# Cached MLA latents: read from a second, host-turned copy page by page, in place of turning them on TensorE

## The reference, cut to what matters

```python
past_c = cache_kv_latent[l][page_table].reshape(Bd, past_len, KV_LORA)   # 8 x 2048 x 128
past_r = cache_k_rope[l][page_table].reshape(Bd, past_len, A_ROPE)       # 8 x 2048 x 32
q_lat = einsum('bqhd,chd->bqhc', q_nope, w_uk)
s_past = (einsum('bqhc,bkc->bhqk', q_lat, past_c)
          + einsum('bqhr,bkr->bhqk', q_rope, past_r)) * scale
p = softmax(concat([s_past, s_new]))
o_lat = einsum('bhqk,bkc->bqhc', p[..., :P], past_c) + einsum('bhqk,bkc->bqhc', p[..., P:], c_new)
```

## Time and profile before

| | |
|---|---|
| median of 3 runs | 2114.58 us (2110.43 to 2116.58) |
| the profiled execution's own time | 2110.66 us |
| its span, first to last instruction | 2108.9 us |
| mean granted clock of PE | 0.995 |
| PE busy, of the span | 2081.8 us (99%) |
| DVE busy | 1573.1 us (75%) |
| ACT busy | 1285.1 us (61%) |
| DMA engines' mean rate | 228 GB/s |

### The profile page before, as it was taken

The page is one execution under the profiler, slowest core; times in us unless marked ns, Lnnn a source line. Parts: engine busy times, 40 slices in busy tenths (PEclk is TensorE's granted clock), DMA queues, the critical chain, the costliest instruction groups (busy, mean ns, idle before and its releaser), DMA issues.

```text
span 2108.9 us, 40790 instructions
## 1 busy us (share of the span) xinstructions
PE 2081.8 (99%) x15576; PEld 1804.4 (86%) x15576; DVE 1573.1 (75%) x3566; ACT 1285.1 (61%) x2523; POOL 124.7 (6%) x138
## 2 busy tenths in 40 slices
PE   9999999999999999999999999999999999999998
PEld 7766699999999888788886667999999998887886
DVE  6873589967899776676577735898688997766666
ACT  5354445568888655565563544456588886655664
POOL 2200010000000010100022000100000001101000
PEclk9999999999999999999999999999999999999999
DMA  9443337776666898898764434477766668988786
GB/s 321 150 156 120 141 109 255 248 252 224 213 220 217 274 311 293 301 323 273 239 223 161 145 121 161 138 255 249 252 214 218 220 208 299 313 289 293 260 265 217
DMA packets 141841, 481.77 MB, mean 228 GB/s; under 512 B 26034, under 2 KB 48594, under 8 KB 135232
## 3 DMA queue, kind: packets, MB, share of 16 engines
q1 hardware_dynamic: 129248, 438.45, 62.3%
q0 software_dynamic: 10496, 40.42, 5.5%
q10 hardware_dynamic: 1904, 0.29, 0.1%
HBM read 475.82 MB, written 104.21 MB: 275 GB/s over the span
## 4 chain that ended last, share of the span: by engine, by line
PE 97%; DVE 2%; DMA 1%; issue 0%; ACT 0%; SPq 0%; DVEq 0%; ACTq 0%
PE ps L1172 35%; PE ps L1219 33%; PE ps L863 4%; PE ps L823 3%; PE ps L907 3%; PE ps L1184 3%; PE ps L1135 2%; PE ps L915 2%; PE ps L1143 1%; PE ps L1139 1%; PE ps L872 1%; PE ps L853 1%; PE ps L1019 1%; PE ps L1158 1%; PE ps L1003 1%; PE ps L1006 1%
## 5 line engine op out<-in xcount | busy, mean ns | idle before, releaser
L2142 DVE TENSOR_TENSOR parts<-region,parts 128x1024 fp32r<-128x1024 f32 x512 | 625.4, 1222 | 302.5 <-ACT parts L1465 300.3
L1172 PE MATMUL ps<-tokens_hi,parts 128*128 128x256 f32 x4096 | 760.5, 284 | 0.0
L1465 ACT CAST parts<-region 128x1024 fp32r<-128x1024 f32 x512 | 538.7, 1052 | 271.2 <-PE ps L1219 213.2
L1219 PE MATMUL ps<-parts,parts_hw 128*128 128x512 f32 x3072 | 699.6, 389 | 0.0
L1219 PEld LDWEIGHTS ps<-parts,parts_hw 128*128 128x128 f32 x3072 | 575.8, 188 | 125.9 <-DVE parts_hw L2192 6.9
L1172 PEld LDWEIGHTS ps<-tokens_hi,parts 128*128 128x128 f32 x4096 | 636.7, 188 | 1.0 <-issue 0.5
L1172 PE MATMUL ps<-parts_hw,parts 128*128 128x256 f32 x2048 | 573.8, 280 | 0.0
L1172 PEld LDWEIGHTS ps<-parts_hw,parts 128*128 128x128 f32 x2048 | 386.5, 189 | 0.0
L1511 ACT ACTIVATE big<-ps 128x256 f32<-128x256 f32 (+31 forms) x252 | 131.6, 522 | 147.0 <-PE ps L1172 147.0
L1499 ACT CAST parts_hw<-big 128x256 fp32r<-128x256 f32 x256 | 171.3, 669 | 0.7 <-DVE big L2203 0.7
L1492 ACT ACTIVATE region<-region 128x128 f16<-128x128 f16 x512 | 169.3, 436 | 0.0
(11 more groups left out here) (324 smaller groups left out, 2247.4 us busy)
## 6 DMA issues: line engine op xcount, KB each, us to landing
region<-in_peer_uT SPq DMA_DIRECT2D x256, 512.0 KB, 4.1
region<-in_peer_v SPq DMA_DIRECT2D x256, 512.0 KB, 4.7
out<-in_state_win_k SPq DMA_DIRECT2D x112, 384.0 KB, 4.9
out<-in_state_win_v SPq DMA_DIRECT2D x112, 384.0 KB, 5.0
big<-in_state_win_k SPq DMA_DIRECT2D x48, 192.0 KB
big<-in_state_win_v SPq DMA_DIRECT2D x48, 192.0 KB, 4.1
region<-in_w_out SPq DMA_DIRECT2D x4, 2048.0 KB, 8.8
big<-in_peer_wq SPq DMA_DIRECT2D x4, 2048.0 KB, 14.2
```

Of the source, the lines that this page charges most:

```text
L1172: mm = pe.matmul(ps[:, j % ZB, 0:SEQ], a, hp[b][:, c, :], start=(c == 0 and n == 0), stop=(c == KD - 1 and n == 2))
L1219: mm = pe.matmul(ps[:, 2 * half + t, :], w_t[a][:, 128 * t:128 * t + 128], v_t[b][:, 512 * half:512 * half + 512], start=(j == 0 and n == ...
L1465: act.copy(hi_t[n % HIGHS], rows_t[n % ROWS]).then_inc(high[l], 1)
L2142: dve.tensor_tensor(lo_t[n % ROWS], rows_t[n % ROWS], hi_t[n % HIGHS], ALU.subtract).then_inc(low[l], 1)
```

## The change

The host adds one input, `cache_latentT`: the cached latents of both layers once more, each page turned to 128 channels by 128 positions (positions in the order in which the gather lays them out), 64 KB to a page. PE no longer turns latents and ACT no longer copies them: the jobs "cT" are gone from all engines. In their place SP loads the turned pages. The physical page number is data, so for each of the 16 pages of each sample SP reads one word of the page table from SBUF into a register (`value_load`), computes the address from it and issues a DMA of 128 rows of 512 bytes.

SP loads samples 0 and 1 before `w_ukT`, sample 2 and half of 3 before the first window keys, and the rest in halves between the window keys. The window values of samples 2 to 7 move behind the last turned page. Ten SBUF areas of 2048 columns now hold turned and unturned latents in rotation, so the turned pages of samples 5, 6 and 7 and POOL's gathers of samples 4 to 7 wait for PE to finish with an earlier sample, and the gathers of samples 2 and 3 take the place at which POOL gathered the second half before. Semaphores of later stages are shared, with their counts raised. Nothing changes in the expert stage.

```diff
-            jobs += [(("cT", b, g), "A") for g in range(4)] + [(("rT", b), "A")]
+            jobs.append((("rT", b), "A"))
...
-        cT = region[:, O_HT:O_HT + 2048].rearrange("p (g k) -> p g k", g=4)
+        pool_a = [past[:, i].rearrange("p g c -> p (g c)") for i in range(4)]
+        pool_b = [region[:, a:a + 2048] for a in (4096, 6144, 0, 2048, O_HT)]
+        turned_at = (pool_a[1], pool_a[2], pool_b[2], pool_b[3], pool_b[4], pool_b[2], pool_b[1], pool_b[4])
...
                 load_w(4)
+                def load_turned(b, g0, g1):
+                    for g in range(g0, g1):
+                        page = sp.value_load(pages[8 * g:8 * g + 1, b:b + 1], min_val=0, max_val=n_phys - 1)
+                        src = A["cache_latentT"][bass.ds(l * n_phys + page, 1)].rearrange("o c t -> (o c) t")
+                        sp.dma_start(turned_at[b][:, PAGE * g:PAGE * g + PAGE], src).then_inc(turned_ld[l][b], 16)
+
+                load_turned(0, 0, NPG)
+                load_turned(1, 0, NPG)
                 sp.wait_ge(product[now[0]], W_LAST[4])
                 sp.dma_start(ukT, L("w_ukT", l)).then_inc(uq_ld, 16)
+                load_turned(2, 0, NPG)
+                load_turned(3, 0, 8)
...
                 def load_vw(b):
                     if b >= 2:
-                        sp.wait_ge(product[now[0]], NUM["ol", (1152 * (b - 1) - 1) // 2048] + 1)
+                        sp.wait_ge(product[now[0]], NUM["ol", b // 4] + 1)
...
                 wait_moved(sp, "qrS")
                 load_kw(0)
                 sp.wait_ge(q_ready, 1)
+                load_turned(3, 8, NPG)
+                load_kw(1)
+                load_turned(4, 0, 8)
+                load_kw(2)
+                load_turned(4, 8, NPG)
+                load_kw(3)
                 load_vw(0)
                 load_vw(1)
-                for b in (1, 2, 3):
-                    load_kw(b)
                 load_kw(4)
-                load_vw(2)
+                sp.wait_ge(product[now[0]], NUM["SC", 2] + 1)
+                load_turned(5, 0, 8)
                 load_kw(5)
-                load_vw(3)
-                load_vw(4)
+                load_turned(5, 8, NPG)
                 load_kw(6)
-                load_vw(5)
-                load_vw(6)
+                sp.wait_ge(product[now[0]], NUM["ol", 2] + 1)
+                load_turned(6, 0, 8)
                 load_kw(7)
-                load_vw(7)
+                load_turned(6, 8, NPG)
+                sp.wait_ge(product[now[0]], NUM["SC", 4] + 1)
+                load_turned(7, 0, NPG)
+                for b in range(2, NB):
+                    load_vw(b)
...
+                for b, free in ((4, ("SC", 3)), (5, ("ol", 3)), (6, ("SC", 5)), (7, ("ol", 4))):
+                    pool.wait_ge(product[now[0]], NUM[free] + 1)
+                    load_past(b, "cache_kv_latent", erow_v_ld[b])
...
-                    for g in range(4):
-                        turn("cT", b, g, parts=[(past_of[b][:, 4 * g + i, :], 128, 128, 128 * i) for i in range(4)])
...
+                    pe.wait_ge(turned_ld[l][b], 16 * NPG)
                     for g in range(4):
-                        pe.matmul(o[32 * g:32 * g + 32, :], qlS[:, b, :], cT[:, g, :], start=True, stop=False, skip_group_check=True)
+                        pe.matmul(o[32 * g:32 * g + 32, :], qlS[:, b, :], pastT_of[b][:, 4 * g:4 * g + 4], start=True, stop=False, skip_group_check=True)
...
-                        for g in range(4):
-                            o = read("cT", b, g)
-                            if b >= 1 and g == 0:
-                                act.wait_ge(product[now[0]], NUM["SC", b - 1] + 1)
-                            act.copy(cT[:, g, :], o[:, 0:512]).then_inc(moved_a[now[0]], 1)
```

More of the change, by code:

```diff
@@ L339, in program @@
         owS2 = PPs.rearrange("p s c k -> p (s c k)")[:, 0:384]
-        past_of = [past[:, b] for b in range(4)]
-        past_of += [region[:, a:a + 2048].rearrange("p (g c) -> p g c", g=NPG) for a in (4096, 6144, 0, 2048)]
+        pool_a = [past[:, i].rearrange("p g c -> p (g c)") for i in range(4)]
+        pool_b = [region[:, a:a + 2048] for a in (4096, 6144, 0, 2048, O_HT)]
+        past_of = [x.rearrange("p (g c) -> p g c", g=NPG) for x in (pool_a[0], pool_a[3], pool_b[1], pool_b[0], pool_b[3], pool_b[0], pool_b[2], pool_b[3])]
+        turned_at = (pool_a[1], pool_a[2], pool_b[2], pool_b[3], pool_b[4], pool_b[2], pool_b[1], pool_b[4])
+        pastT_of = [x.rearrange("p (g t s) -> p t g s", g=NPG, s=8) for x in turned_at]
+        n_phys = A["cache_kv_latent"].shape[1]
         vw_of = [vw[:, b] for b in range(2)]
@@ L405, in program @@
         sk_ld = sem("subkeys_loaded")
-        wq_ld = [sem(f"query_weights_loaded{i}") for i in range(4)]
+        wq_ld = [sem(f"turned_latents_then_query_weights{i}") for i in range(4)]
         pw_high = sem("product_weights_high")
@@ L451, in program @@
         w_mul = sem("late_weights_multiplied")
-        row_ld = [[ctx.enter_context(nc.semaphore(f"u_or_v_loaded{k}_{i}")) for k in range(ROWS)] for i in range(DEPTH)]
+        row_ld = [[ctx.enter_context(nc.semaphore(f"turned_latents_then_u_or_v{k}_{i}")) for k in range(ROWS)] for i in range(DEPTH)]
+        turned_ld = [row_ld[i] + wq_ld[0:3] for i in range(DEPTH)]
         h_high = sem("tokens_high")
@@ L471, in program @@
         past_ld = ctx.enter_context(nc.semaphore("past_loaded"))
-        pastb_ld = ctx.enter_context(nc.semaphore("past_second_half_loaded"))
         pastr_ld = ctx.enter_context(nc.semaphore("past_second_half_rope_loaded"))
         erow_u_ld = [ctx.enter_context(nc.semaphore(f"u_rows_gathered{b}")) for b in range(NB)]
-        erow_v_ld = [ctx.enter_context(nc.semaphore(f"v_rows_gathered{b}")) for b in range(NB)]
+        erow_v_ld = [ctx.enter_context(nc.semaphore(f"latents_then_v_rows{b}")) for b in range(NB)]
         rows_ready = ctx.enter_context(nc.semaphore("past_rows_ready"))
@@ L735, in load_past @@
                                             A[name].rearrange("l n (s t) c -> (l n s) (t c)", s=8), row).then_inc(done, 16)
-                for b in range(4):
+                for b in range(2):
                     load_past(b, "cache_kv_latent", past_ld)
@@ L758, in _ @@
                 pool.wait_ge(product[now[0]], W_LAST[4])
-                for b in range(4, NB):
-                    load_past(b, "cache_kv_latent", pastb_ld)
+                for b in (2, 3):
+                    load_past(b, "cache_kv_latent", erow_v_ld[b])
                 pool.wait_ge(qk_ready, 1)
@@ L1240, in _ @@
                             o_y = begin("gy")
-                        pe.wait_ge(erow_v_ld[b - 1], l * 16 + 16)
-                        pe.wait_ge(erow_v_ld[b], l * 16 + 16)
+                        for r in (b - 1, b):
+                            pe.wait_ge(erow_v_ld[r], (l * 32 + 32) if r >= 2 else (l * 16 + 16))
                         for half in range(2):
@@ L1439, in query_high @@
                     if p == 0:
-                        act.wait_ge(wq_ld[i], 16)
+                        act.wait_ge(wq_ld[i], 16 * NPG + 16 if i < 3 else 16)
                     c = slice(1024 * p, 1024 * p + 1024)
@@ L2336 @@
         "state_convT": s.transpose(0, 4, 3, 1, 2),
+        "cache_latentT": arrays["in_cache_kv_latent"].reshape(-1, 8, PAGE // 8, LAT).transpose(0, 3, 2, 1).reshape(-1, LAT, PAGE),
         "peer_subkeysT": arrays["in_peer_subkeys"].reshape(DEPTH, NSUB, NK, P).transpose(0, 3, 1, 2),
```

11 lines of the change are left out of this document (7 added, 4 removed).

## The result

The changed kernel takes 2182.28 us (median of 4 runs, 2176.93 to 2190.38) against 2115.58 for the kernel before (4 runs, 2110.43 to 2119.59). The ratio is 1.032, with a 95% interval of 1.028 to 1.0359: 3.2% slower. The forecast was 2152, the range 2092 to 2195. One execution of the kernel with constant page numbers took 6052.86 us; the median given for it counts this execution (without it, 2103.78 instead of 2104.49), the ratio doesn't.

The account below looks back on a forecast made before the run. PE was taken to bound the kernel, DVE second, and SP's page loads to make the change slower: 2110.66 + 30.7 (SP's delay) + 6.8 (clock) = 2148.2 us, forecast as a median of 2152, range 2092 to 2195.

Parts of the forecast that it names:

- The cost of a page: On SP, c = 0.33 (DMA issue) + 3 x 0.058 (small instructions) + 0.55 (register load) = 1.05 us; bounds 0.65 and 2.5.
- the sum: 2110.66 (profiled execution) + 30.7 (SP's delay) + 6.8 (clock) = 2148.2 us; forecast median 2152, 37.5 slower.
- The delay of the last score: Sample 7's score on PE needs all 128 pages: 128c - 119.7 us late in layer 0, 128c - 118.4 in layer 1; together 30.7.
- The clock term, 6.8 us: PE, waiting several us in a step, loses clock: one such stretch added to each layer, 6.8 us in all.
- Rival C: Pace as forecast, but PE stays at the low clock through the loop: 15 to 20 us more a layer, about 2185; chance 0.08.
- `w_ukT` late above c = 0.91: On SP, 32 pages stand ahead of `w_ukT`, issued at 71.50 us before: late as soon as c is over 0.91 us.
- What the turns are worth, 10 us in a layer: PE loses 28.8 us of turns, but gains only until DVE is never idle: at most 11.7 us a layer, taken as 10.
- Rival A: Register load under 0.35 us, c under 0.85: DVE is the bound, 20 us faster, a median of 2095; chance 0.36.
- POOL: "nothing": Gathers of samples 2 to 7 are later, but issued at least two steps ahead of their mix: no cost.
- Break-even at 0.93: Gain and loss cancel where 256c - 238.1 is nothing: c = 0.93 us a page, register load 0.43.
- The transfers follow SP's pace and aren't the limit: On the DMA engines, a page takes 0.55 us of all 16, less than c, so transfers aren't the limit.
- The expert stage: A sign that the forecast is right: the expert stage takes what it took.

Follow-up runs that it names:

- The run at 0.88: The changed kernel with the bounds test of each page number left out, 0.88 us a page: 2123.62 us, ratio 1.001 to the kernel before.
- the last experiment: Against the kernel with late gathers, the gather of sample 4's latents also waits until sample 5's keys have landed: 2100.64 us, ratio 0.9917 to the kernel before.

## Why the prediction was right, and where its size was off

The direction and the mechanism were right: SP's register work per page, not PE, sets the end of the loop. That the time lies in the range says less, since 2092 to 2195 held a gain of 20 us as well as a loss of 80; the forecast of 37.5 us slower was little more than half of what came. By the steps of the prediction:

- **The cost of a page.** Forecast 1.05 us, in the trace 1.167 on the average of the 256 pages. This is the mis-sized term. The profiled executions lie 71.6 us of span apart and the sum had 37.5, so it was 34.1 short; by 256 pages this term is 30.0 of them. The register load itself, which the text took to be the unknown, was less than chosen: 0.27 instead of 0.55. What was too small was "three small register instructions" at 0.058 each, gap included. There are four (the two fused ones, the assertion, the move), and with their gaps and those around the load and the DMA they take 0.50. The fused one of the bounds test alone takes 0.152. This makes the plain page of 1.11 us shown above; the average is higher, among other things because 37 of the 256 loads took over 0.44 us. A price read off 63 semaphore clears in a row isn't that of another kind of instruction.
- **The Trainium skill's floor for a `tensor_load`** ("DMA: Bandwidth & Descriptors", "Latency and other measured facts": about 600 ns). The trace doesn't agree: 0.27 us for a load of one register on SyncE at the median and 0.262 at least, 0.53 for eight; the measurement decides. The page adds that the compiler unrolls by default to amortize the load. No run here unrolls; the load by the row spreads its cost in another way. By the floor the sum would have come out nearer for the wrong reason, since the load costs less than half of it, and the other instructions more than the text had.
- **The delay of the last score, 128c - 119.7 and 128c - 118.4.** At the 1.156 and 1.179 of the two layers these give 28.3 and 32.5; measured 31.1 and 36.8. The rest, 2.8 and 4.3 us, is in SP's rows: its 24 key issues took 13.1 and 12.9 us instead of 10.3, one group of three up to 3.05, and it waited 0.7 and 2.2 us until DVE had read the key buffer. The last page landed sooner than the sum had it and gives some of this back.
- **The clock term, 6.8 us.** After the two loops' 67.9 us 3.7 remain of the 71.6: layer 0's end is 1.6 us less late than its score, layer 1's 5.2 more. So some 3.7 at most, 3.1 less than the sum had (30.0 + 2.8 + 4.3 - 3.1 = 34.0, the shortfall). The experiment with the turns put back in the changed kernel can't separate the clock from the added work. Rival C, which had the low clock as a cost of its own, came out at the right time (2185), and the clock was low in the loop as it said (0.76 from 100 to 215 us). But SP's rows account for the loops and leave its cost no room: that the number came out is luck.
- **`w_ukT` late above c = 0.91.** Right (7.8 us late in the changed kernel, on time at 0.88), and worth nothing, which the prediction didn't say: it stands ahead of the same queue.
- **What the turns are worth, 10 us in a layer.** Right as a number, shown only once SP and the keys were on time: 2096.61 without, 2116.79 with. The way to it, DVE never idle, wasn't. In the changed kernel the turns are worth about nothing.
- **Rival A** (2095 us if a page is cheap). Its mechanism is real. At 0.54 and 0.59 us a page the time was 2104.49 and 2105.64, because the step **POOL: "nothing"** was wrong: with the moved gathers beside them the last keys of layer 0 were in flight 8.45 and 8.84 us instead of 4.19. With the gathers behind the keys, 2096.61. In the changed kernel itself this error didn't count, since SP was later than everything else.
- **Break-even at 0.93.** The run at 0.88 was level with before, 1.001. Its last scores began at 182.06 and 1230.43, 4.2 and 8.1 us later than in the earlier trace rows, though by 128c - 119.7 they were not late. In its layer 0 DVE waits 1.7 to 5.8 us for the keys of four samples; those of three stand behind pages, and those of two have gathers beside them; how the two share the loss isn't shown.
- **The transfers follow SP's pace and aren't the limit.** Right: with constant page numbers the same number of bytes moved at 0.54 us a page.
- **The expert stage** is unchanged, the two largest groups of PE 760.5 and 699.6 us in both kernels.

## What to carry to other kernels

A load that is addressed by data costs the issuing engine instructions, and on SyncE these stand in one line with every other transfer: multiply the cost per item by the count and set it against the deadline of the last item, as above. Load the numbers by the row and test their bounds elsewhere; here that turned 3.2% slower into 0.6% faster, most of it by leaving out the test. When an operation leaves the bottleneck, look at which transfers have moved with it: the next limit was gathers of 1 MB under way beside transfers of 192 KB that had no slack. And when a wait is cured and the time stays, look where the wait went.

## What the runs showed of the hardware that was not expected

- On SyncE a register load takes 0.27 us at the median for one register, 0.53 for eight, 0.97 to 0.99 for sixteen in seven of eight cases. Single ones took up to 1.17 us for one register; that one (at 1159.32 in the changed kernel) followed right on a page's DMA, and its cause isn't shown. A fused register instruction takes 0.04 to 0.05 us for an address and 0.152 for the bounds test, an assertion 0.018, a move 0.029, and between two instructions there are 0.03 to 0.05 us.
- The issue of a DMA with its address in a register costs SyncE no more than a constant one: 0.337 us at the median against 0.33, plus 0.08 us of a fused instruction and a move and the gaps around them. With constant page numbers, one issue right behind the other, the same copies took 0.433 us at the median (0.327 at least), so a page there costs 0.54 and not the 0.38 that was expected; why isn't shown.
- The last keys (three transfers of 192 KB) were in flight 4.19 us in layer 0 of the kernel before with no gather beside them, 8.45 and 8.84 beside two gathers of 1 MB. In layer 1 it was 5.37 and 6.40 with the gathers and 3.03 without. A flight can also be long without such a gather beside it: 6.70 us for the keys of sample 4 in layer 1 of the last experiment.
